# PEER gates in an RWKV-7/MLA/PEER kernel: the gate product stored packed as the moving operand, the first one-hot read as strided weights without a packing copy

## The reference

```python
s1, i1 = lax.top_k(s[:, :, 0], PEER_TOPK)          # 16 of 128 keys, first half of the query
s2, i2 = lax.top_k(s[:, :, 1], PEER_TOPK)          # 16 of 128 keys, second half
...
cand_e = (i1[..., :, None] * PEER_N_KEYS + i2[..., None, :])
top_s, top_pos = lax.top_k(cand_s, PEER_TOPK)
experts = jnp.take_along_axis(cand_e, top_pos, axis=-1)
gate = jax.nn.softmax(top_s, axis=-1)
act = jax.nn.gelu(jnp.einsum('thkd,td->thk', u_tab[experts], xb))
return jnp.einsum('thk,thkd->td', gate * act, v_tab[experts])
```

## Time and profile before

| | before |
|---|---|
| median of 3 runs | 3272.99 us (3272.36 to 3275.35) |
| the profiled execution | 3266.96 us, its span 3265.2 us |
| PE busy | 2851.1 us, 87% |
| DVE busy | 1882.5 us, 58% |
| ACT busy | 1119.7 us, 34% |
| POOL busy | 282.0 us, 9% |
| mean granted TensorE clock | 0.924 of full speed |

### The profile page before, as it was taken

How to read it: one execution, slowest core, us unless ns; L and a number is a source line. 1 busy time by engine, 2 the same in 40 slices (tenths; PEclk the granted TensorE clock), 3 DMA queues, 4 the chain that set the end, 5 groups by cost and what they waited for, 6 DMA issues and landing times.

```text
span 3265.2 us, 60101 instructions
## 1 busy us (share of the span) xinstructions
PE 2851.1 (87%) x22131; PEld 2596.3 (80%) x22131; DVE 1882.5 (58%) x3520; ACT 1119.7 (34%) x2050; POOL 282.0 (9%) x377
## 2 busy tenths in 40 slices
PE   6845667999999999997569999976799999999998
PEld 5634555899999999996348888861589999999998
DVE  2265553698889655541533444452169888955554
ACT  1222210244444444441123444430024444444443
POOL 0013210000111000000001111112000011100000
PEclk9968977999999999998768999996799999999999
DMA  4300001354444455554001222225245444445554
GB/s 151 116 18 21 15 9 55 119 181 153 143 143 147 156 180 180 181 188 167 0 1 41 58 58 58 58 62 150 83 131 181 149 145 145 143 162 181 181 181 139
DMA packets 112351, 377.98 MB, mean 116 GB/s; under 512 B 14569, under 2 KB 24042, under 8 KB 111538
## 3 DMA queue, kind: packets, MB, share of 16 engines
q1 hardware_dynamic: 88562, 322.17, 29.5%
q0 software_dynamic: 13248, 43.98, 4.5%
q10 hardware_dynamic: 10368, 9.44, 1.0%
HBM read 371.52 MB, written 4.01 MB: 115 GB/s over the span
## 4 chain that ended last, share of the span: by engine, by line
PE 71%; issue 15%; DVE 9%; ACT 2%; DMA 1%; ACTq 1%; DVEq 0%; SPq 0%; POOLq 0%; POOL 0%
PE ps L709 69%; DVE arena L1215 3%; ACT arena L1836 2%; DVE arena L1219 1%; DMA arena<-in_cache_n 1%; PE ps L959 1%; PE ps L746 1%; DVE arena L1599 1%; DVE arena L1590 1%; ACTq L529 1%; DVE arena L1229 0%; ACTq L530 0%; DVE ring_lo L1215 0%; DVE arena L1594 0%; PE ps L965 0%
## 5 line engine op out<-in xcount | busy, mean ns | idle before, releaser
L1215 DVE TENSOR_TENSOR ring_lo<-ring,w_hi 128x1024 fp32r<-128x1024 f32 x512 | 625.8, 1225 | 457.5 <-ACT w_hi L1836 451.7
L1836 ACT ACTIVATE arena<-ps 128x264 f32<-128x264 f32 (+18 forms) x1021 | 413.7, 424 | 1249.9 <-PE ps L709 1083.6
L709 PE MATMUL ps<-arena 64*64 64x64 f32 (+11 forms) x5228 | 570.1, 297 | 187.2 <-DVEq L1212 62.2
L709 PEld LDWEIGHTS ps<-arena 64*64 64x64 f32 (+6 forms) x5228 | 444.0, 166 | 303.6 <-issue 74.2
L1836 ACT ACTIVATE w_hi<-ring 128x1024 fp32r<-128x1024 f32 x512 | 541.8, 1059 | 390.6 <-PE ps L709 390.2
L709 PE MATMUL ps<-x_hi,w_hi 128*128 128x264 f32 x2048 | 595.0, 291 | 15.5 <-DVE ring_lo L1215 15.5
L709 PE MATMUL ps<-h_hi,w_hi 128*128 128x264 f32 x2048 | 580.1, 283 | 6.8 <-DVE ring_lo L1215 6.8
L709 PE MATMUL ps<-x_lo,w_hi 128*128 128x264 f32 x2048 | 584.9, 286 | 0.0
L709 PE MATMUL ps<-x_hi,ring_lo 128*128 128x264 f32 x2048 | 583.8, 285 | 0.0
L709 PE MATMUL ps<-h_lo,w_hi 128*128 128x264 f32 x2048 | 582.3, 284 | 0.0
L709 PE MATMUL ps<-h_hi,ring_lo 128*128 128x264 f32 x2048 | 582.1, 284 | 0.0
(11 more groups left out here) (164 smaller groups left out, 2281.2 us busy)
## 6 DMA issues: line engine op xcount, KB each, us to landing
ring<-in_wstream SPq DMA_DIRECT2D x608, 512.0 KB, 3.3
arena<-in_cache_t POOLq DMA_DIRECT2D x128, 192.0 KB, 2.6
arena<-in_cache_n ACTq DMA_DIRECT2D x72, 128.0 KB, 2.7
arena<-in_cache_n POOLq DMA_DIRECT2D x56, 128.0 KB, 2.8
arena<-in_mla_w POOLq DMA_DIRECT2D x1, 3072.0 KB, 10.2
arena<-in_state POOLq DMA_DIRECT2D x4, 512.0 KB, 4.2
out_wkv_s<-arena POOLq DMA_DIRECT2D x4, 512.0 KB, 3.9
arena<-in_consts SPq DMA_DIRECT2D x1, 1408.0 KB
```

Of the source, the lines that this page charges most:

```text
L709: return nc.tensor.matmul(out, lhsT, rhs, start=start, stop=stop, **kw)
L1215: return v.tensor_tensor(out, a, b, op)
L1836: return nc.scalar.activation(out, in_, func, **kw)
```

## The change

In the order of the diff: the one-hot buffers shrink from five to four planes of 128 x 4 fp16 values. The copy `oh1c` and POOL's loop `gate_rows` are gone, with both semaphores. PE reads the weights straight from `oh1`, one value in every four, so 8 bytes apart. `oh2g` is stored with the token outside: the 128 values of a token and part are adjacent, 256 bytes per token. DVE still runs through it with the token innermost, so successive values that it writes are 256 bytes apart. PE reads the moving operand packed.

```diff
-        oh1c = [a[:, 2 * OHT * P:3 * OHT * P].rearrange("p (u n) -> p u n", u=OHT) for a in oh]
-        oh2g = [a[:, 3 * OHT * P:].rearrange("p (k n u) -> p k n u", k=2, u=OHT) for a in oh]
+        oh2g = [a[:, 2 * OHT * P:].rearrange("p (k u n) -> p k u n", k=2, u=OHT) for a in oh]
...
-            def gate_rows(layer):
-
-                for i in range(NSETS):
-                    pool.wait_ge(oh1_made, NSETS * layer + i + 1)
-                    nc.gpsimd.tensor_copy(oh1c[i % OHS], oh1[i % OHS].rearrange("p n u -> p u n")).then_inc(oh1_ready, 1)
-
...
-                    pe.wait_ge(oh1_ready, s0 + i + 1)
                     pe.wait_ge(oh2g_made, s0 + i + 1)
                     for u in range(OHT):
                         for k in range(2):
-                            last = mm(ps[:, b, u * P:(u + 1) * P], oh1c[st][:, u, :], oh2g[st][:, k, :, u], k == 0, k == 1)
+                            last = mm(ps[:, b, u * P:(u + 1) * P], oh1[st][:, :, u], oh2g[st][:, k, u, :], k == 0, k == 1)
...
-                    tt(oh1[st], keys8, these(0, 1).broadcast_to([P, P, OHT]), ALU.is_equal).then_inc(oh1_made, 1)
+                    tt(oh1[st], keys8, these(0, 1).broadcast_to([P, P, OHT]), ALU.is_equal)
                     tt(oh2[st], keys8, these(1, 1).broadcast_to([P, P, OHT]), ALU.is_equal).then_inc(oh2_made, 1)
                     dve.wait_ge(oh2_made, s0 + i + 1)
-                    tt(oh2g[st], oh2[st].unsqueeze(1).broadcast_to([P, 2, P, OHT]),
+                    tt(oh2g[st].rearrange("p k u n -> p k n u"), oh2[st].unsqueeze(1).broadcast_to([P, 2, P, OHT]),
```

More of the change, by code:

```diff
@@ L180, in build @@
         OH_AT = W_AT + WHI * D
-        oh_words = OHT * 5 * P // 2
+        oh_words = OHT * 4 * P // 2
         KEY_AT = OH_AT + 2560
@@ L472, in build @@
         sel_ready = sem("sel_ready")
-        oh1_ready = sem("oh1_ready")
         oh_used = sem("oh_used")
-        oh1_made = sem("oh1_made")
         oh2_made = sem("oh2_made")
@@ L655, in _ @@
             pool.wait_ge(st_out, 64)
-            gate_rows(0)
             pool.wait_ge(x_added, 2)
@@ L681, in _ @@
                     page(pool, cache_n, it * NSLOT + n, cpN[n], natp_in[n])
-            gate_rows(1)
             pool.wait_ge(x_added, 4)
```

## The result

| | before, on the same chip | after |
|---|---|---|
| median | 3272.68 us (3266.22 to 3275.35) | 3678.99 us (3669.28 to 3680.42, 4 runs) |
| ratio | | 1.124 [1.121, 1.126] |
| span of the profiled execution | 3265.2 us | 3667.5 us |

The kernel became 12.4% slower, 406 us, where the prediction had 39 us and a range up to 3370. The direction was right and the size was off by a factor of ten.

What follows compares the result with a forecast made beforehand. PE was taken as the bound, DVE close second. Per layer 64 x 0.85 = 54.4 us added on DVE, less 32.8 and 2.15 us of room, gives 19.4; both layers 39 us, so 3312 us, range 3268 to 3370.

Steps and rivals of the forecast that it cites:

- How the product is written: DVE's product, writing 256 bytes apart: 0.64 ns per value on top of 1225 ns, so 0.85 us more per product.
- the first rival: DVE's product has no far-write penalty and takes 1225 ns, PE's sets get shorter: 3238 us; chance 0.14.
- The sum: DVE's added time, 64 x 0.85 = 54.4 us, less 32.8 and 2.15 us of room: 19.4 us per layer.
- the room: DVE's idle time before PE must wait for it: 32.8 us before `lower`, plus 2.15 us at the end.
- the end: From last product to PE's last hidden tile: 8.9 us available, 6.75 needed, so 2.15 us of room per layer.
- The removed copy: POOL's packing copy holds up DVE's product by about 0.36 us per set; PE never waits for the copy.
- PE's operands: PE's 8 gate matmuls per set, moving operand read packed: 0.37 us less per set.
- The rival by which the sets would stay at 0.84 us: No penalty on DVE and nothing gained on PE, the moving stride not being its limit: 3273 us; chance 0.08.
- A dearer far write: DVE's product at 1.06 ns per value, 1.29 us more each: 95 us in all, 3368 us; chance 0.15.
- A falling clock: PE's clock falls because PE waits up to about 1.2 us per step; included in the dearer case, chance 0.15.

Runs made afterwards that it cites:

- run 4: Kernel before, with nineteen DVE products of 1024 values behind its last output, varying write step and type, the row run twice; 3374.75 us with this row.
- Run 6: Turned-round product kernel (run 2) plus one unused operation of 512 packed f32 values behind each product; 3292.12 us, ratio 1.007 to the kernel before.
- run 1: Changed kernel, no copy and weights read strided, but the product back in its old layout, token innermost; 3278.79 us, ratio 1.0026 to the kernel before.
- run 5: Kernel before, keeping POOL's copy and packed weights, with only the product written packed by the turned loop and read packed; 3264.63 us, ratio 0.9988.
- run 2: Changed kernel with DVE's product loop turned round, key innermost: adjacent writes, reads 8 bytes apart; 3229.89 us, ratio 0.9876 to the kernel before.
- run 8: Kernel before plus DVE and ACT probes behind its end: 1024 fp16 values in runs of adjacent ones, copies, bf16; runs of one 4.72 us, two 1.08.

## Why the prediction was wrong

**The step that failed** is "How the product is written", and in it one choice: "I take 0.85 us: L1727 is itself a far write by DVE, and the far read gives the same price". All of the earlier trace rows are f32. The prediction said so itself under the first rival ("no row shows a far write of 2-byte values, all are f32"), and used that only as a reason for a cheaper write, never for a dearer one. The prediction added its price to the 1225 ns of an f32 operation, at 0.64 ns per value. On that base the product of the kernel after shows 3.46 ns per value (4772 less 1225, over 1024), and run 4 shows 0.66 for 4 bytes beside it. The upper bound of 1.06 ns per value was from f32 rows too, and so the range was a range of the wrong quantity. Measured in the kernel, the term was 3.75 us per product (4772 less 1019) instead of 0.85.

**The sum** was right in its form. With what the rows of after show, the three instructions grow by 3.79 us (5.59 for 1.80), the next one begins 0.39 us before their record ends (911.67 for 912.06) where it was 0.08 (791.83 for 791.91, at the first set), and `lower` takes 1.34 us to the next start instead of 1.15 (909.80 less 908.65 in the trace of before). Added per step: 3.79 - 0.31 + 0.19 = 3.67 us. All 66 products count now, not 64, since the first ones already keep PE waiting: 66 x 3.67 = 242, less the room of 34.95, gives 207 us per layer. From the first one-hot to the first output the stretch of layer 0 grew from 297.80 us (790.09 to 1087.89) to 500.38 (787.65 to 1288.03), by 202.6. The 4 us between them are in the step, which I took from single rows. From the first one-hot to the last product DVE's busy time is this:

```profile
790.09:1075.41 285.32, 285.32 (x2384) 281.82 (x2383) 248.99 (x414) 121.39 (x295) 51.24 (x66) 1.00 0.43 144
787.65:1276.45 488.80, 336.35 (x2401) 322.98 (x2399) 484.10 (x414) 127.62 (x298) 0.00 (x0) 0.84 0.25 86
```

It grows from 248.99 to 484.10, by 235.1 us or 3.56 per set. DVE's waits for ACT fall from 32.9 us to 2.4, which leaves 204.6, and 203.5 were measured (285.32 to 488.80). The time behind the last product is 0.9 us shorter. The mechanism, its place and the room (30.5 us of waits, where 32.8 were counted) are as predicted. So is the end, but for the clock: layer 1, where it stayed full behind the last product, gained 2.4 us there (2.15 predicted). Run 6 tests the same sum with a dose that has nothing to do with far writes.

**The removed copy** was priced at 0.36 us of DVE; run 1 shows 0.327 and run 5 0.330. The Trainium skill (SBUF — State Buffer, "Who interferes with whom") has a rule by which GpSimd and a two-input VectorE operation lock a shared port against each other, and these numbers agree with it.

**PE's operands** were priced at 0.37 us less per set. Measured: 0.41 (0.43 for 0.84). Taken apart: packing the moving operand gives 0.42 (run 1 to run 2: 0.87 to 0.45), and reading the weights 8 bytes apart costs 0.02 to 0.03. The rival by which the sets would stay at 0.84 us falls. Its rule in the Trainium skill (SBUF — State Buffer, on cachelines), that two hits on a 16-byte line give full bandwidth, does not hold here for the moving operand: 8 bytes apart 105 ns per matmul, packed 54. It does not hold for DVE's fp16 writes either: 8 bytes apart they take 2.43 us, packed 0.69, and 1.23 with a packed write at the slower rate (run 2). For f32 writes it does: 8 bytes apart 1.23 us, packed 1.22.

**The rivals.** The one with the rate of f32 on DVE (3238 us) did not come true, but run 2, one turned loop away, gives 3230 by just this mechanism. "A dearer far write" had the right sign and a bound three times too low (1.06 ns per value for 3.46). A falling clock did come (0.81 to 0.87), and cost nothing where PE waited anyway, and 1.5 us at the end of layer 0.

**What stays open.** The width of the write decides, but how the price arises is not shown: why 8 bytes apart cost half of 16 bytes, why runs of two values still cost 0.39 us more than packed, and why a copy pays half of what a product pays. Open is also why the hidden tiles take 0.02 us longer in run 1. A product that writes runs of four values (0.69 us in run 8, with both operands read packed) might take DVE out of the way in the last groups of run 2 as well. Its gate operand would have a step of zero, which that probe had not, and it was not tried.

## What to carry to other kernels

When the walk of an operation goes across the layout, put the strided side on the read and keep 2-byte results adjacent, at least in pairs (run 8: 1.08 us for 4.72). Here the same elements took 4.77 us one way round and 1.22 the other, and that decided between 12% slower and 1.2% faster. A price read off rows holds for their element width: before it is carried over to fp16, ask what a row of f32 can't show, and let the range reach upward for it. A copy that is hidden may still slow the engine beside it, and this costs nothing until that engine becomes the bound (run 1 against run 5).

## What was not expected of the hardware

- In a two-input product on DVE, lone 2-byte results cost 4.4 to 4.7 us per 1024 from 16 bytes apart on, at every pitch tried from 256 to 320 bytes; on ACT it is 4.75 at 16 bytes. At 8 bytes apart DVE takes 2.43 us. 4-byte results take 1.90 to 1.99 us for the same, and a pair of 2-byte results 1.08.
- The instruction behind a far write is slower too: `lower` takes 1.34 us to the next start there (911.67 to 913.01) and 1.15 in the kernel before.
- The moving operand of an fp16 matmul read 8 bytes apart takes 105 ns for 128 columns, packed 56 (0.45 us for 8 in run 2), both at a granted clock of 1.00. Weights read 8 bytes apart make it 3 ns longer (run 1).
- A `tensor_scalar` with two values per partition takes 0.22 us from start to start for 128 fp16 values (8 in 1.88 us behind one another in run 8), with one value 0.16 to 0.17 (8 in 1.39 us).
